# The two rings of split weights, moved 20 bytes further in SBUF

## Reference, cut to what matters

```python
def swiglu(h, w_in, w_out):
    g, u = split_cols(h @ w_in, (D_FF, D_FF))
    return (jax.nn.silu(g) * u) @ w_out
...
    for layer in range(DEPTH):
        g = ln_gains[layer]
        x = x + 0.5 * swiglu(rms_norm(x, g[0]), ffn1_w_in[layer], ffn1_w_out[layer])
        h = rms_norm(x, g[1])
...
        x = x + mixed
        x = x + memory_cross_attention(rms_norm(x, g[2]), rms_norm(mem, g[3]), x_w_q[layer],
                                       x_w_kv[layer], x_qk_gains[layer], x_w_o[layer])
        x = x + 0.5 * swiglu(rms_norm(x, g[4]), ffn2_w_in[layer], ffn2_w_out[layer])
```

## Time and profile before

| | |
|---|---|
| median of 3 runs | 2406.56 us |
| the runs | 2395.4, 2406.56, 2407.18 us |
| profiled execution, its own time | 2406.13 us |
| its span, first to last instruction | 2404.3 us |
| busy: TensorE | 2291.9 us (95%) |
| busy: weight loads (PEld) | 2197.9 us (91%) |
| busy: VectorE | 1537.7 us (64%) |
| busy: ScalarE | 1184.5 us (49%) |
| busy: GpSimd | 129.8 us (5%) |
| mean granted TensorE clock | 0.978 |

### The profile page before, as it was taken

How to read it: one execution, slowest core, us unless ns; L and a number is a source line. 1 busy time by engine, 2 the same in 40 slices (tenths; PEclk the granted TensorE clock), 3 DMA queues, 4 the chain that set the end, 5 groups by cost and what they waited for, 6 DMA issues and landing times.

```text
span 2404.3 us, 44793 instructions
## 1 busy us (share of the span) xinstructions
PE 2291.9 (95%) x18446; PEld 2197.9 (91%) x18446; DVE 1537.7 (64%) x2216; ACT 1184.5 (49%) x1747; POOL 129.8 (5%) x146
## 2 busy tenths in 40 slices
PE   6999998889999999998999999998999999998998
PEld 6999876879999999787999999986999999998998
DVE  5766647566666765776666666667665666666664
ACT  5644434555446544445554544444544544426543
POOL 2000000110001001000100000100100000001001
PEclk9999987899999999999999999999999999999999
DMA  7556422326555557343455655642655565543653
GB/s 236 190 180 185 149 70 93 106 88 198 184 189 184 189 185 228 106 144 120 141 194 183 196 183 180 219 141 72 192 184 182 180 191 180 162 141 106 194 188 110
DMA packets 383369, 393.27 MB, mean 164 GB/s; under 512 B 6512, under 2 KB 381424, under 8 KB 383040
## 3 DMA queue, kind: packets, MB, share of 16 engines
q1 hardware_dynamic: 381248, 383.30, 49.9%
q0 software_dynamic: 1920, 7.11, 1.0%
HBM read 389.34 MB, written 1.05 MB: 162 GB/s over the span
## 4 chain that ended last, share of the span: by engine, by line
PE 87%; DVE 6%; ACT 4%; issue 1%; POOL 1%; DMA 1%; SPq 0%; POOLq 0%; ACTq 0%; DVEq 0%
PE acc L531 25%; PE acc L535 25%; PE acc L532 24%; PE wide L674 2%; PE acc L549 2%; PE acc L551 2%; PE acc L550 2%; ACT w_hi L815 1%; PE wide L647 1%; DVE w_lo L1048 1%; DVE hn_lo L1080 1%; POOL t L1432 1%; PE wide L663 1%; DMA raw<-in_ffn_w_in 1%; PE wide L602 1%
## 5 line engine op out<-in xcount | busy, mean ns | idle before, releaser
L815 ACT ACTIVATE w_hi<-raw 128x1024 fp32r<-128x1024 f32 (+1 forms) x742 | 768.7, 1040 | 963.8 <-PE acc L535 864.2
L1048 DVE TENSOR_TENSOR w_lo<-raw,w_hi 128x1024 fp32r<-128x1024 f32 (+1 forms) x742 | 889.2, 1201 | 536.1 <-ACT w_hi L815 533.2
L531 PE MATMUL acc<-hn_hi,w_hi 128*128 128x256 f32 x3536 | 855.7, 283 | 37.3 <-DMA colc<-in_cols 18.3
L532 PE MATMUL acc<-hn_lo,w_hi 128*128 128x256 f32 x3536 | 846.2, 280 | 0.0
L531 PEld LDWEIGHTS acc<-hn_hi,w_hi 128*128 128x128 f32 x3536 | 671.2, 190 | 50.7 <-DMA colc<-in_cols 18.3
L532 PEld LDWEIGHTS acc<-hn_lo,w_hi 128*128 128x128 f32 x3536 | 671.5, 190 | 0.5
L535 PE MATMUL acc<-hn_hi,w_lo 128*128 128x256 f32 x3536 | 482.1, 279 | 0.0
L535 PEld LDWEIGHTS acc<-hn_hi,w_lo 128*128 128x128 f32 x3536 | 442.2, 189 | 0.0
L531 PE MATMUL acc<-hid_hi,w_hi 128*128 128x256 f32 x1408 | 334.5, 278 | 0.0
L532 PE MATMUL acc<-hid_lo,w_hi 128*128 128x256 f32 x1408 | 334.5, 278 | 0.0
L532 PEld LDWEIGHTS acc<-hid_lo,w_hi 128*128 128x128 f32 x1408 | 265.3, 188 | 0.0
(11 more groups left out here) (199 smaller groups left out, 2036.4 us busy)
## 6 DMA issues: line engine op xcount, KB each, us to landing
raw<-in_ffn_w_in SPq DMA_DIRECT2D x88, 1024.0 KB, 5.1
raw<-in_ffn_w_out SPq DMA_DIRECT2D x32, 1024.0 KB, 5.2
raw<-in_ffn_pre_w_gate SPq DMA_DIRECT2D x22, 1024.0 KB, 5.3
raw<-in_ffn_pre_w_up SPq DMA_DIRECT2D x22, 1024.0 KB, 5.3
raw<-in_ffn_post_w_gate SPq DMA_DIRECT2D x22, 1024.0 KB, 5.3
raw<-in_ffn_post_w_up SPq DMA_DIRECT2D x22, 1024.0 KB, 5.3
raw<-in_x_w_kv SPq DMA_DIRECT2D x16, 1024.0 KB, 5.4
raw<-in_ffn_pre_w_down SPq DMA_DIRECT2D x16, 1024.0 KB, 5.1
```

The source lines that it names most:

```text
L531: nc.tensor.matmul(bank, wh[:, j, :], a_hi[:, u.k0 + j, :], start=u.first and j == 0, stop=False)
L532: nc.tensor.matmul(bank, wh[:, j, :], a_lo[:, u.k0 + j, :], start=False, stop=False)
L815: nc.scalar.activation(w_hi[:, u.slot, 0:u.nk, :], raw[:, u.raw % RING, 0:u.nk, P * u.half:P * u.half + P], ACT.Copy).then_inc(w_hi_ready, 1)
L1048: nc.vector.tensor_tensor(w_lo[:, u.slot, 0:u.nk, :], raw[:, u.raw % RING, 0:u.nk, P * u.half:P * u.half + P], w_hi[:, u.slot, 0:u.nk, :]. ...
```

## The change

The two rings are no longer tensors of their own but two parts of one tensor that has five more words ahead of them. `w_hi` begins at byte 90,324 and `w_lo` at 106,708 of each partition, 20 bytes further than before: multiples of 4 bytes, but not of 8, 16 or 32. The slots keep their size and order, so each slot, block and run of weights is moved by the same 20 bytes. What follows the rings moves by 32 bytes (`t1` to 123,104, and so on), and what lies ahead of them, `raw`, the activations `hn_*` and `mn_*`, stays. The one tensor is called `split_w` in a profile, where `w_hi` and `w_lo` stood, and lines behind L206 have a number that is higher by one. On every engine the instructions, their order, shapes and waits are those of before; only addresses differ.

```diff
         raw = sb("raw", [P, RING, 8, CW])
         apart = sb("apart", [P, 16])
-        w_hi = sb("w_hi", [P, RING, 8, P], F32R)
-        w_lo = sb("w_lo", [P, RING, 8, P], F32R)
+        split_w = sb("split_w", [P, 5 + 2 * RING * 8 * P], F32R)
+        w_hi, w_lo = (split_w[:, 5 + i * RING * 8 * P:5 + (i + 1) * RING * 8 * P].rearrange("p (s k n) -> p s k n", s=RING, k=8)
+                      for i in range(2))
         t1 = sb("t1", [P, KB, T])
```

## The result

The changed kernel takes 2468.63 us (median of 4 runs, 2466.13 to 2470.35), the kernel before 2404.52 us (4 runs, 2395.4 to 2407.18). The ratio is 1.0273 with a 95% interval of 1.0243 to 1.0303: slower by 2.7%, just above the range that was given, and on the other side of "no change".

A forecast was written before the change was run, and what follows sets the result against it. TensorE was taken as bound by weight loading and streaming alike, with no slack. Every part of the change was priced at 0, so 2406.13 us + 0 = 2406 us; range 2366 to 2464 us.

The forecast's parts named there:

- What bounds the kernel: TensorE: bound by loading weights and by streaming alike, no slack; a load x ns longer costs x ns per matmul.
- weights as the stationary operand: Weight loads of 16,368 mode F matmuls: 0 extra, read word by word; bounds 0 and 1670 us.
- The line rival: Every mode F weight load pays for a newly touched line: 2461 us, or 2419 at one word's time; chance 0.17.
- The rival that named the meeting of two reads in SBUF: TensorE matmuls: moving one operand against the other fixes the slower pace, adding 37 us, 2443; chance 0.08.
- Its other sign: TensorE matmuls: the same mechanism fixes the faster pace, 2406 - 37 = 2369 us; chance 0.13.
- What moved behind the rings: Everything allocated behind the rings moves by 32 bytes, each start still a multiple of 32: cost zero.
- Mode T at 0: 1056 matmuls with weights as the moving operand: 0 extra, with less confidence than for loads; bounds 0 and 113 us.
- the rival's prices: Mode T moving operand read in broken pairs: 56 us for half extra, 113 us at half rate; chance 0.06.
- VectorE and ScalarE at 0: VectorE reading w_hi and writing w_lo, ScalarE writing w_hi at new addresses: 0, with cover behind TensorE.

The follow-up runs named there:

- only_lo_odd: Against the kernel before: w_hi stays at 90,304, w_lo alone begins 20 bytes further, hid moves by 32 bytes; 2430.13 us, ratio 1.0083.
- acts_108_further: Against the kernel before: activations hn and mn begin 108 bytes further, everything behind them 128 bytes further; 2448.32 us, ratio 1.016.
- rings_64_back: Against the kernel before: the rings begin 64 bytes earlier, nothing else moved; 2480.7 us, ratio 1.0292.
- odd_rings_alone: Against the kernel before: the rings begin 12 bytes earlier, nothing behind them moved; 2392.7 us, ratio 0.9916.

## Why the prediction was wrong

**What bounds the kernel: right.** TensorE's pace times 17,424 matmuls gives 62 of the 63 us, and a few nanoseconds a matmul were not hidden by anything. That the load by itself needs as long as the matmul was read from plain float32 rows; no run tests it for these weights.

**The failed step: weights as the stationary operand, taken at 0, "since the load goes word by word".** The load's own record agrees: 188 ns before and after. The step looked at one operand's start and asked whether it is odd. What the runs showed in its place is that the start of the weights and the start of the stream act together on the distance between matmuls, which a load's record does not show: 84 bytes past a multiple of 128 with the stream at 0 is 120.0 ns, the same with the stream at 32 is 113.6 ns. The term was 12,144 x 4.3 ns = 52 us. The bounds that I set were 0 and 1670 us; the measured value is near the low one. That the two paces of before are also 4.3 ns apart is a coincidence as far as the runs show.

**The rivals.** The line rival gave 2461 us, the closest number, by the wrong mechanism, which is luck: an extra line would cost at 52 as at 84, and cost nothing at 80. The rule on lines of the Trainium skill ("SBUF — State Buffer", section "Door 1: The DMA port swizzle (why [64,N] ≈ [32,N])") asks for two hits in a line, which contiguous 4-byte words give in every line but a last one with a single word. The count of lines does not order the times here: 33 lines at 52 went at 113.7 ns, 32 lines at 80 at 118.9. The rival that named the meeting of two reads in SBUF, one operand moved against the other, is the one that the runs leave standing, though none of them shows where the two meet. I priced it as one of the two paces already seen, 37 us, and gave it 0.08 and 0.13. A third pace was possible and came. Its other sign exists too: two layouts stay at 113.3 to 113.7 ns in mode F and end at 0.992. My argument against it, that the pace changes while the addresses stay, was wrong: the addresses shift which paces occur, and something else picks among them. The Trainium skill also says, in the section "Who interferes with whom" of "SBUF — State Buffer", that TensorE's two read ports, for the stream and for the weights, are independent. If that is read as the one never slowing the other, these runs do not agree: with the weights in place, a move of the stream by 64 bytes took 115.7 ns to 119.9. Whether it is at the ports or elsewhere that they meet is not shown.

**What moved behind the rings, at 0: wrong by mechanism, small here.** hid moved by 32 bytes, which put it at another distance from the rings than hn. That fits its 4224 matmuls losing 0.8 ns and not 4.3; had it stayed, at distance 84, I would expect of it what hn shows, but no kernel tried that. That a move behind the rings can cost by itself is seen in only_lo_odd, where w_hi stayed and hid moved: its L531 and L532 went from 115.6 to 118.3 ns, above both paces of before.

**Mode T at 0: mis-sized.** 1056 x 6.0 ns = 6 us, where 56 and 113 us were the rival's prices. The means of the five matmul groups show it too; L550 was L549 of the earlier trace rows, at 285 ns:

```profile
L550 PE MATMUL acc<-split_w,hn_hi 128*128 128x256 f32 x224 | 65.7, 293 | 4.6 <-DVE split_w L1049 4.6
```

**VectorE and ScalarE at 0: right.** +4 ns and +2 ns an instruction, hidden.

**What holds over all kernels tried.** Take the distance from the start of the stream to that of the weights, past a multiple of 128. Where the stream starts at a multiple of 32 bytes, the mode F paces go with it (cases counted by kernel and operand; only_lo_odd, with two distances at once, is left out):

- 64: 113.3 or 117.8 ns (ten cases).
- 52: 113.3 to 113.7 ns in five cases, and a mix of 113.4, 117.8 and 120.0 in one, hid of the changed kernel.
- 0: 119.9 to 120.0 ns (three); 36: 120.0 (two); 84: 120.0 (one).
- 56: a mean of 117.8 (two).
- Once each: 96, 80 and 68 with hn, means of 118.3, 118.9 and 118.3; 48 with hid, 118.6.

Where it starts 12, 16 or 20 bytes past one, the list fails in three of four kernels: distance 64 gave 120.0, distance 52 gave 118.1 and 118.9. Only acts_108_further, at 84, fits. What in the memory makes it so is not shown, nor what picks a pace where several are possible, nor a layout that is good for mode T as well. The best two versions, 2392.7 and 2391.39 us, beat both kernels; that they are ahead by the mode F pace and give back some 6 us in mode T (1056 x 5.6 ns) is worked out from the table.

## What to carry to other kernels

In this kernel, where TensorE loads weights and streams back to back almost all the time, the places of the two operands in SBUF were worth between 0.8% gained and 2.9% lost, and aligned starts did not guard against the bad ones. How much it is elsewhere was not measured. Before an edit that moves buffers is called neutral, look at the distance between starts of matmuls, and when a kernel slows down or speeds up by a few per cent after an unrelated change of allocation, look there first. A comparison of two layouts needs several executions, because one layout can hold two paces: the same kernel before ran in 2395.4 to 2425.02 us.

## What the runs showed of the hardware that was not expected

TensorE's pace in a stream of float32r matmuls of 256 columns has steps at full clock: 113.3, 117.8, 118.3 and 120.0 ns in mode F and 121.7, 122.1 and 123.3 ns in mode T were each held to a few tenths over hundreds of matmuls. Other numbers of the table, 118.9 among them, are means of mixed paces. At the granted clock of 0.50 there is one pace, 213 to 214 ns: before, after, and in rings_64_back, the slowest kernel, where 14 loads from 38.17 to 41.16 us are 213.6 ns each. There the layout costs nothing. At distance 64 the pace is either 113.3 or 117.8 ns, each for a whole stage as a rule, and the same stage had the one in one execution and the other in the next. The rings at a multiple of 128 bytes with the activations also at one was the slowest of all layouts tried, at 1.0292. And a single weight load shows little of it. With hid as the stream its record is 188 ns before, after and in odd_rings_alone, at mean paces from 113.3 to 116.4 ns; in rings_64_back, at 120.0 ns throughout, the groups of weight loads have

```profile
L530 PEld LDWEIGHTS acc<-hid_hi,split_w 128*128 128x128 f32 x1408 | 270.3, 192 | 0.0
```

and with hn 193 to 194 ns, where it is 189 to 190 before and after, although hn goes at 120.0 ns after as well. So the record of the load, 4 to 5 ns longer there, is not the pace; only the distance from one start to the next is.
